# Two decoder blocks in one program: an early half tile in the second feed-forward, neighbourhood attention's first units moved among differential attention's last steps, and the residual loaded tile by tile

## The reference

```python
h = rmsnorm(x, pre_mix_w); proj = h @ w_in
y_a = diff_attention(q_a, k_a, v_a, lam, subln_w, lambda_init)   # 4 heads, two softmax maps each
y_b = neighbourhood_attention_2d(q_b, k_b, v_b, rpb)             # 8 heads, 8 x 16 window on a 16 x 64 grid
merged = g_a * (y_a @ w_branch_a) + g_b * (y_b @ w_branch_b)     # g_a, g_b: sigmoid gates from proj
x = x + rmsnorm(merged @ w_out, post_mix_w)
h = rmsnorm(x, pre_ffn_w)
f = (silu(h @ w_gate) * (h @ w_up)) @ w_down                     # inner width 2816 = 22 tiles of 128
x = x + rmsnorm(f, post_ffn_w)
```

## Time and profile before

| | |
|---|---|
| median of 3 runs | 2957.29 us (2957.23 to 2958.44) |
| the profiled execution's own time | 2958.75 us |
| its span, first to last instruction | 2956.9 us |
| PE busy | 2868.3 us, 97% of the span |
| DVE, ACT, POOL busy | 1393.5, 957.4, 369.7 us |
| mean granted TensorE clock | 0.991 |
| transfers over the span | 270.01 MB, mean 91 GB/s |
| chain of waits | PE 83%, DVE 8%, ACT 3%, issue 2%, DMA 2%, POOL 1% |

### The profile page before, as it was taken

One profiled execution on the slowest core, in us unless ns is written; L12 is line 12 of the kernel. 1 busy time (PEld: TensorE's weight loads), 2 busy tenths in 40 slices (PEclk: granted clock), 3 DMA queues, 4 the chain that ended last, 5 costly groups with the idle time before them and its releaser, 6 DMA issues.

```text
span 2956.9 us, 31552 instructions
## 1 busy us (share of the span) xinstructions
PE 2868.3 (97%) x13108; PEld 2322.7 (79%) x13108; DVE 1393.5 (47%) x1660; ACT 957.4 (32%) x1255; POOL 369.7 (13%) x333
## 2 busy tenths in 40 slices
PE   8999999999999999999999999999999999999997
PEld 6877668888888888788878887667777888888886
...
GB/s 116 79 79 137 145 65 109 49 39 61 42 52 40 61 36 54 93 142 185 162 72 98 107 93 78 192 203 167 210 118 56 41 57 39 61 36 58 43 61 118
DMA packets 88655, 270.01 MB, mean 91 GB/s; under 512 B 12600, under 2 KB 17336, under 8 KB 88512
## 3 DMA queue, kind: packets, MB, share of 16 engines
...
## 4 chain that ended last, share of the span: by engine, by line
PE 83%; DVE 8%; ACT 3%; issue 2%; DMA 2%; POOL 1%; DVEq 0%; SPq 0%; ACTq 0%; POOLq 0%
PE ps L211 82%; DVE cacc L182 1%; ACT PB L176 1%; PE ps L214 1%; POOL ga L179 1%; DVE PB L182 1%; DVE ps L191 1%; DVE YA L179 1%; DVE sqacc L179 1%; DVE YA L182 0%; DVE XT L179 0%; DMA xin<-in_xT 0%; DMA raw<-in_w_w2out 0%; ACT wh L176 0%; DVE AL L182 0%
## 5 line engine op out<-in xcount | busy, mean ns | idle before, releaser
L211 PE MATMUL ps<-AH,wh 128*128 128x512 f32 (+1 forms) x2232 | 887.5, 398 | 38.1 <-DVE wl L179 13.3
L211 PE MATMUL ps<-AH,wl 128*128 128x512 f32 (+1 forms) x2232 | 871.7, 391 | 0.0
L211 PE MATMUL ps<-AL,wh 128*128 128x512 f32 (+1 forms) x2232 | 871.2, 390 | 0.0
L179 DVE TENSOR_TENSOR wl<-raw,wh 128x1024 fp32r<-128x1024 f32 (+2 forms) x227 | 269.4, 1187 | 808.7 <-ACT wh L176 808.6
L211 PEld LDWEIGHTS ps<-AH,wh 128*128 128x128 f32 (+1 forms) x2232 | 418.8, 188 | 140.1 <-DVE AL L182 15.4
L176 ACT ACTIVATE wh<-raw 128x1024 fp32r<-128x1024 f32 (+2 forms) x274 | 252.5, 922 | 766.4 <-PE ps L211 754.2
L211 PEld LDWEIGHTS ps<-AH,wl 128*128 128x128 f32 (+1 forms) x2232 | 418.6, 188 | 91.1
L211 PEld LDWEIGHTS ps<-AL,wh 128*128 128x128 f32 (+1 forms) x2232 | 419.0, 188 | 88.3 <-issue 2.9
L211 PE MATMUL ps<-UH,wh 128*128 128x512 f32 (+1 forms) x840 | 325.2, 387 | 0.0
L211 PE MATMUL ps<-UL,wh 128*128 128x512 f32 (+1 forms) x840 | 325.1, 387 | 0.0
L211 PE MATMUL ps<-UH,wl 128*128 128x512 f32 (+1 forms) x840 | 325.1, 387 | 0.0
...
## 6 DMA issues: line engine op xcount, KB each, us to landing
...
```

The source lines that it names most:

```text
L179: return Issued(self, self.e.tensor_tensor(out, a, b, op))
L211: return Issued(self, self.e.matmul(out, l, r, start=start, stop=stop))
```

## The change

Three parts, each in its own stage.

1. **Neighbourhood attention among differential attention's last steps.** PE issues units 0 and 1 between steps 3 and 4 of the last gate half, turns unit 31 only after gate step 6, then gate step 7 and units 2 and 3, and puts the first `rows(0)` ahead of the last two of `value(15)`'s eight products. DVE takes the maxima of units 0 and 1 between `joined(31)` and its copy. ACT runs the last exponentials ahead of the copy of gate half 30, and the last sigmoid ahead of `copied(15)`. SP issues the table `tabS` of head 0 during u = 30, and the keys table `tabT` and head 0's `km` loads ahead of head 1's queries and keys and ahead of `y_store(15)`. `add(0)` and `add(1)` no longer wait for the stores of `s_ya`.
2. **The residual tile by tile.** The eight loads of `AL` stand one behind each of the first eight weight loads of `out2`, instead of all eight ahead of them. The first product waits for merged product 7 (`wbe`) instead of 8.
3. **An early half tile.** Gate 1's first half goes into `pe_out2`, between up 0's first half and the second halves. Its weights are kept in `UH2[5]`, `UL2[5]` (`G1`). The stage's norm is split into two halves of four token blocks: norm 6 aside of up 0 and gate 1, norm 7 aside of gate 1's second half and up 1. Later norms are numbered one higher. The first evacuations become half wide (`first2`).

The diff, cut to what the parts above and the prediction speak of:

```diff
@@ -94,7 +96,7 @@
     out = []
-    staged = [TILE["gu", ("g", 0)], TILE["gu", ("u", 0)]]
+    staged = [TILE["gu", ("g", 0)], TILE["gu", ("u", 0)], G1]
     for s, (name, key, _) in enumerate(TILES):
@@ -103,8 +105,8 @@
         elif s == staged[0]:
-            out += [(staged[0], 0), (staged[1], 0), (staged[0], 1), (staged[1], 1)]
-        elif s != staged[1]:
+            out += [(t, half) for half in range(2) for t in staged]
+        elif s not in staged:
             out += [(s, 0), (s, 1)]
@@ -426,6 +428,8 @@
             return self.wlast[s - LAST8]
+        if s == G1:
+            return self.UH2[:, 5, :], self.UL2[:, 5, :]
         if s == WB2:
@@ -436,6 +440,8 @@
             q.wait_ge(self.S.mx, 192)
+        elif s == G1:
+            q.wait_ge(self.S.gem, GEM_END[TILE["w2out", (1, 7)]])
         elif s >= 2:
@@ -1819,9 +1827,17 @@
                 value(u // 2 - 1)
-            turn(u)
-            self.gate_steps(q, u, 4, 8 if u < 31 else 5)
-        value(15)
+            if u < 31:
+                turn(u)
+                self.gate_steps(q, u, 4, 8)
+        for u in range(2):
+            self.na_unit(q, u)
+        self.gate_steps(q, 31, 4, 7)
+        turn(31)
+        self.gate_steps(q, 31, 7, 8)
+        for u in (2, 3):
+            self.na_unit(q, u)
+        value(15, lambda kb: self.na_rows(q, 0) if kb == 6 else None)
@@ -1864,13 +1880,14 @@
                 self.w_high(q, TILE["w2in", ("g", u // 2)] + 1)
+            if u == 30:
+                exps(31)
             gate_half(u)
-            if u < 31:
+            if u < 30:
                 exps(u + 1)
-                if u % 2:
-                    gate(u // 2)
+            if u % 2:
+                gate(u // 2)
         copied(15)
-        gate(15)
@@ -1915,6 +1932,9 @@
                 maxes(u + 1)
+            else:
+                self.na_most(q, 0)
+                self.na_most(q, 1)
             copies(u)
@@ -1958,13 +1978,15 @@
                         self.na_qk(q, 0)
+            if u == 30:
+                self.na_tab(q, 0)
             if u % 2 == 0 and u:
...
                 self.w_load(q, TILE["w2in", ("g", u // 2)] + 3)
-        self.na_tab(q, 0)
+        self.na_km(q, 0)
+        self.na_tab_keys(q, 0)
         self.na_qk(q, 1)
-        self.na_km(q, 0)
         y_store(15)
@@ -2060,8 +2082,8 @@
         self.na_tabled(q, h, 1)
-        q.wait_ge(S.tr, 64)
-        q.wait_ge(S.cc, 32)
+        q.wait_ge(S.tr, 64 if h else 62)
+        q.wait_ge(S.cc, 32 if h else 31)
         q.wait_ge(S.tad, 12 * (h - 1))
@@ -2087,34 +2109,38 @@
+    def na_unit(self, q, u):
...
+        self.na_loaded(q, h, 1)
+        q.wait_ge(S.mx, 128 if u < 2 else 128 + u - 1 if u < 4 else 128 + u)
...
+    def na_rows(self, q, g):
...
@@ -2278,19 +2299,21 @@
+    def na_most(self, q, u):
...
+        q.wait_ge(S.sc, 128 + u + 1)
+        self.na_tabled(q, h, 1)
...
@@ -2307,8 +2330,9 @@
             q.wait_ge(S.tpv, 64 + n - 3)
-            q.wait_ge(S.dya0, 128)
-            q.wait_ge(S.dya1, 128)
+            if n >= 2:
+                q.wait_ge(S.dya0, 128)
+                q.wait_ge(S.dya1, 128)
             q.wait_ge(S.dg0, 128)
@@ -2481,7 +2505,6 @@
-        self.na_tab_keys(q, 0)
         self.na_tab(q, 1)
@@ -2622,24 +2645,33 @@
         def stats5(half, k):
-            if k == 6:
+            if k == 4:
                 q.wait_ge(S.pa, 21)
...
         def rows5(half, k):
-            if k == 2:
+            if k == 0:
                 self.norm_rows(q, 5, self.rcols[:, 12:16], 4, 8)
+            if k == 4:
+                q.wait_ge(S.xacc, 14)
+                self.norm_stats(q, 6, self.acc3, 0, 4)
+        def rows6(half, k):
+            if k == 4:
+                q.wait_ge(S.nrb, 4)
+                self.norm_rows(q, 6, self.rc8[:, 0:4], 0, 4)
...
                 x = 8 * half + n
-                q.wait_ge(S.wbe, 8)
+                q.wait_ge(S.wbe, 7 if x == 0 else 8)
                 q.wait_ge(S.ps, 8 + x - 3)
...
         self.half_product(q, u0, self.Ah, self.Al, 8, 0, 2, P, None, None, True, True, rows5)
+        self.half_product(q, G1, self.Ah, self.Al, 8, 0, 6, P, None, None, True, True, rows6)
         for k in range(8):
@@ -2686,10 +2718,21 @@
         self.norm_sqrt(q, 5, 4)
+        self.w_high(q, G1)
         rows(1)
+        self.norm_sqrt(q, 6, 4)
         for n in range(NT):
             x3(n, 1)
-        self.w_high(q, TILE["gu", ("g", 1)])
+            if n == 3:
+                q.wait_ge(S.nrow, 6)
+                q.act(self.RB[:, HALF[0]], self.bank(4), ACT.Copy).then_inc(S.nrb)
+    def first2(self, q, x, half):
+        q.wait_ge(self.S.gem, GEM[TILE["gu", ("g", 0)] + x, half])
+        q.wait_ge(self.S.nrb, 6 + half)
+        t = q.tt(self.cv2[2 * x][:, HALF[half]], self.bank(2 * x + half), self.RB[:, HALF[half]], ALU.mult)
+        t.then_inc(self.S.uev if half else self.S.fuh)
@@ -2741,11 +2784,13 @@
         self.w_low(q, TILE["gu", ("u", 0)])
+        self.norm_recip(q, 5, self.rcols[:, 12:16], 4)
         low(7, 0)
         total(0)
-        self.norm_recip(q, 5, self.rcols[:, 12:16], 4)
+        self.w_low(q, G1)
         mult(0, 1)
         mult(1, 1)
+        self.norm_recip(q, 6, self.rc8[:, 0:4], 4)
         add(0, 1)
@@ -2753,8 +2798,8 @@
             low(n, 1)
+        self.first2(q, 1, 0)
         total(1)
-        self.w_low(q, TILE["gu", ("g", 1)])
@@ -2794,11 +2839,11 @@
         q.wait_ge(S.wba, 7)
-        for n in range(NT):
-            q.dma(self.Al[n], self.io["s_x"][n, :, :]).then_inc(self.load8(n)[0], 16)
         for half in range(2):
                 self.w_load(q, TILE["w2out", (half, n)] + 3)
+                if half == 0:
+                    q.dma(self.Al[n], self.io["s_x"][n, :, :]).then_inc(self.load8(n)[0], 16)
                 if half and n:
@@ -2845,27 +2890,30 @@
-        def norm(half, k):
-            if (half, k) == (0, 5):
+        def stats7(half, k):
+            if k == 6:
                 q.wait_ge(S.xacc, 21)
-                self.norm_stats(q, 6, self.acc3, 0, NT)
-            if (half, k) == (1, 0):
-                q.wait_ge(S.nsq, 6)
-            if (half, k) == (1, 1):
-                self.norm_rows(q, 6, self.rc8, 0, NT)
+                q.wait_ge(S.nrb, 6)
+                self.norm_stats(q, 7, self.acc3, 4, 8, 4)
+        def rows7(half, k):
+            if k == 2:
+                self.norm_rows(q, 7, self.rc8[:, 4:8], 4, 8)
+        q.wait_ge(S.nsq, 6)
+        self.half_product(q, G1, self.Ah, self.Al, 8, 1, 7, P, None, None, True, True, stats7)
+        q.wait_ge(S.fuh, 1)
+        self.half_product(q, G1 + 1, self.Ah, self.Al, 8, 0, 2, P, None, None, True, True, rows7)
+        self.f2_evac(q, 1)
+        self.half_product(q, G1 + 1, self.Ah, self.Al, 8, 1, 3)
         for x, step in enumerate(self.STEPS2):
-            if x < 2:
+            if x < 4:
                 continue
             s = self.f2_tile(step)
-            if x == 2:
-                q.wait_ge(S.nrb, 5)
-                q.wait_ge(S.nsq, 5)
-            else:
-                self.f2_evac(q, x - 2)
+            self.f2_evac(q, x - 2)
             if isinstance(part, str):
-                self.product(q, s, self.Ah, self.Al, 8, self.f2_pair(x), P, None, None, norm if x == 2 else None)
+                self.product(q, s, self.Ah, self.Al, 8, self.f2_pair(x))
             else:
...
@@ -2965,32 +3013,35 @@
+        def gated(i):
+            cv = self.cv2[2][:, :]
+            q.wait_own()
+            q.wait_ge(S.usl, 22 + i + 1)
+            q.tt(cv, cv, self.cv2[i % 2][:, :], ALU.mult).then_inc(S.umul)
...
@@ -3019,9 +3070,11 @@
         self.w_low(q, TILE["gu", ("u", 1)])
-        self.norm_recip(q, 6, self.rc8, 8)
-        evac(0)
-        evac(1)
+        self.first2(q, 0, 0)
+        self.norm_recip(q, 7, self.rc8[:, 4:8], 4)
+        self.first2(q, 0, 1)
+        self.first2(q, 1, 1)
+        gated(0)
         end = len(self.STEPS2) - 1
@@ -2176,24 +2202,19 @@
-        for u in range(4):
-            unit(u)
-            if u < 3:
-                self.gate_steps(q, 31, 5 + u, 6 + u)
-        rows(0)
         for n in range(99):
...
                 if u is not None:
-                    unit(u)
+                    self.na_unit(q, u)
                 branch(2 * n)
...
                 if g is not None:
-                    rows(g)
+                    self.na_rows(q, g)
         branch(192)
```

116 lines of the change are left out of this document (56 added, 60 removed).

## The result

| kernel | time, median (range, runs) | ratio to before, 95% interval |
|---|---|---|
| before | 2957.26 us (2956.84 to 2958.44, 4) | |
| after | 2938.02 us (2936.73 to 2939.80, 4) | 0.9943 (0.9929 to 0.9957) |
| after, again, on another chip | 2936.54 us (2932.19 to 2938.89, 6), before there 2955.00 | 0.9939 (0.9926 to 0.9952) |

The prediction was 2940.0 us (2934 to 2947): the sum was right within 2 us. The profiled execution of after took 2939.8 us, 18.95 less than that of before. Of that, 2.2 us lie ahead of the first place and 0.7 us behind the first product of the last down tiles, in code that the change does not touch; only 16.0 us lie between, so that the closeness of this first pair to the forecast is in part luck.

A forecast was written before the change was run, and what follows sets the result against it. TensorE, busy 97% of the span, was taken as the bound. Gains of 6.2, 3.5 and 8.5 us sum to 18.2, giving 2940.5 us from the profiled 2958.75 and 2939.1 by the median; predicted 2940.0, range 2934 to 2947.

The forecast's parts named there:

- Place A: Differential to neighbourhood attention: less TensorE idle, earlier first add, less half clock; 6.2 us gained, ends 3.0 and 9.0.
- 3.0 step: Start of neighbourhood attention: TensorE idle before `step(0)` falls from 3.9 to about 0.9 to 1.2 us.
- 1.9 table: Start of neighbourhood attention: with the keys table early, `add(0)` follows `step(0)` by 0.8 instead of 2.72 us.
- 1.3 clock: Ten microseconds at 1.2 GHz from 1849.8: gain between 0 and 4.1 us, taken as 1.3.
- Place B: Residual loads in the output projection: fourth weight tile no longer queued behind them; 3.5 us gained, ends 1.8 and 3.5.
- 1.82 wait: Output projection: TensorE's wait until 2118.01, before the fourth product, goes; 1.82 us.
- 1.7 dip: Output projection, 2119 to 2123: clock at 0.57 right after the wait; its 1.7 us loss goes.
- The first wait for 7 in place of 8: First output projection product waiting for one merged tile fewer: put at nothing, less than 0.3 us either way.
- Place C: Before the second feed-forward: TensorE idle falls from 11.3 to about 3 us; 8.5 us gained, ends 6.5 and 9.5.
- The chain 0.7 later: Before the second feed-forward: DVE's chain starts 0.7 us later because a new reciprocal stands ahead of its first `add`.
- The rival of the clock and the transfers: Start of neighbourhood attention: clock or transfers eat the gain, leaving 3.0 us there; 2943.7 us, chance 0.20.
- The others: Rivals: second feed-forward bound at gate 2, 2943.5 us, 0.08; Place B alone, 2955.2, 0.05; slower through 1.2 GHz clock, 0.03.

The follow-up runs named there:

- e1: The kernel before with only the differential and neighbourhood attention part of the change: 2950.15 us, ratio 0.9977.
- e5: The kernel after, with the first head's keys table again asked for behind differential attention's last store: 2944.75 us in its one run.
- e12: The kernel before with only SyncE's edits, the first head's tables and key-and-mask tile asked for earlier and reordered: 2953.34 us, ratio 0.9991.
- e9: The kernel before with 19 extra products, results overwritten, in TensorE's waits at the start of neighbourhood attention: 2954.06 us, ratio 1.0003.

## Why the prediction was right

- **Place A, 6.2 us** (3.0 step, 1.9 table, 1.3 clock): measured 6.2 by the means of e1, 7.8 by profiles, 3.6 in the first pair. The sum was right, and the step and the table work as forecast: `step(0)` comes 3.64 us earlier against C0 (20.23 and 16.59), where 3.0 were worked out, and `add(0)` 1.97 us closer behind it, where 1.9 were, 5.6 in all. But they are not two gains that can be had one by one: alone they are worth 1.3 and 1.6 (e5, e12). What is left open is how much of the 5.6 lasts to the stage's end and how much is the clock's. Profiles at equal time at 0.50 give 3.7 us for the order, and by the runs' mean clock some 2.9 of e1's 6.2 us go with the clock, more than the 1.3 priced; e9 has the same rise of the clock and gained nothing (at most 2.1 us by its interval), with 19 products more to do. So that 3.0, 1.9 and 1.3 sum to just what was measured is partly luck.
- **Place B, 3.5 us** (1.82 wait, 1.7 dip): measured 2.1 by means and 2.8 by profiles. The wait is exact; the dip was counted as sure and came in two of five profiles without the change. The first wait for 7 in place of 8 was worth nothing, as said.
- **Place C, 8.5 us**: 8.6 in every pair of profiles without a dip, 9.2 with them. The chain 0.7 later was 0.73, no wait at gate 1's evacuation, the last groups' start 0.75 later. That the 0.7 is the difference of a loss of 1.9 and a gain of 1.36 was not seen.
- **The rival of the clock and the transfers** (A worth 3.0, 2943.7 us) looked right on the first pair of profiles alone; by the kernel's time e1 put it aside (at least 4.1 us). The others did not come: no wait at gate 1's evacuation, parts that add up, and each dip of the changed order in A over within 3.4 to 6.8 us (10.2 in e5, with the late table). That rival leaned on a window that its rows do not show, where the clock is back at full:

```profile
1859.80:1866.10 6.30, 4.88 (x23) 2.95 (x22) 2.31 (x8) 3.17 (x8) 0.00 (x0) 1.00 1.05 234
```

- What the prediction did not see is that POOL's sums made six of DVE's operations in that chain 1.1 us slower each, though 1.77 beside 0.68 stood in its own rows; that was worth another 2.9 us.
